# Layer kernel on one core: first values from unnormalised x, GpSimd's factors behind the copies in the sparse pairs, second sum of a norm in two halves

## The reference, cut to what matters

```python
# layer 1 (gated convolution + 16-head dilated attention)
u = rms_norm(h, norm_g)                  # y = x * rsqrt(mean(x*x) + 1e-6) * g
proj = u @ w_in                          # 10 parts of 1024 columns; part 6 is v
h = rms_norm(h + hybrid_mixer(...), final_g)
# layer 2 (12 heads, three sparse branches, and 4 memory heads)
o = gc[..., 0:1] * o_c + gc[..., 1:2] * o_s + gc[..., 2:3] * o_w     # compressed, selected, window
x = layer_norm(ALPHA * x + mix, ln1_g, ln1_b)
x = layer_norm(ALPHA * x + conv_ffn(x, ...), ln2_g, ln2_b)
# layer 3 (12 heads over blocks, 4 memory heads), same two norms
```

## Time and profile before

| | value |
|---|---|
| median of three runs | 958.37 us |
| profiled execution | 958.25 us |
| its span, first to last instruction | 956.6 us |
| TensorE busy | 928.9 us (97%) |
| VectorE busy | 659.4 us (69%) |
| ScalarE busy | 527.2 us (55%) |
| GpSimd busy | 65.6 us (7%) |
| granted TensorE clock, mean | 0.994 |

### The profile page before, as it was taken

The page is one execution under the profiler, slowest core; times in us unless marked ns, Lnnn a source line. Parts: engine busy times, 40 slices in busy tenths (PEclk is TensorE's granted clock), DMA queues, the critical chain, the costliest instruction groups (busy, mean ns, idle before and its releaser), DMA issues.

```text
span 956.6 us, 19717 instructions
## 1 busy us (share of the span) xinstructions
PE 928.9 (97%) x7025; PEld 844.7 (88%) x7025; DVE 659.4 (69%) x1258; ACT 527.2 (55%) x967; POOL 65.6 (7%) x119
## 2 busy tenths in 40 slices
PE   7999999999999999989999999999999999999995
PEld 4899999999999988667899999998988699999995
DVE  6466666666767777985886666668577796666665
ACT  5455555555544567764755455556665565555553
POOL 1000000000000001550100000001000100000001
PEclk9999999999999999999999999999999999999998
DMA  7555555556566666323566555565654447555641
GB/s 240 183 180 190 175 178 183 171 195 225 186 195 191 243 214 200 116 62 110 176 200 240 189 187 194 189 196 174 189 183 158 157 159 237 188 197 185 195 157 44
DMA packets 48233, 172.98 MB, mean 181 GB/s; under 512 B 6032, under 2 KB 6480, under 8 KB 48061
## 3 DMA queue, kind: packets, MB, share of 16 engines
q1 hardware_dynamic: 44732, 159.78, 50.7%
q0 software_dynamic: 3456, 12.61, 4.3%
HBM read 171.29 MB, written 1.07 MB: 180 GB/s over the span
## 4 chain that ended last, share of the span: by engine, by line
PE 86%; DVE 7%; ACT 3%; issue 2%; DMA 1%; POOL 0%; SPq 0%; POOLq 0%; DVEq 0%; ACTq 0%
PE bank L1411 18%; PE bank L1412 18%; PE bank L1410 18%; PE ysum L1481 6%; PE ysum L1483 6%; PE ysum L1482 6%; DVE sb_wl L830 2%; PE bank L1530 1%; PE ysum L1537 1%; PE ysum L1544 1%; PE ysum L1458 1%; PE ysum L1462 1%; PE ysum L1459 1%; DMA sb_raw<-in_stream 1%; ACT sb_xh L463 1%
## 5 line engine op out<-in xcount | busy, mean ns | idle before, releaser
L1411 PE MATMUL bank<-sb_xl,sb_wh 128*128 128x256 f32 x1360 | 377.9, 278 | 0.0
L1412 PE MATMUL bank<-sb_xh,sb_wl 128*128 128x256 f32 x1360 | 375.8, 276 | 0.0
L1410 PE MATMUL bank<-sb_xh,sb_wh 128*128 128x256 f32 x1332 | 370.5, 278 | 1.4 <-DVE sb_wl L830 1.4
L830 DVE TENSOR_TENSOR sb_wl<-sb_raw,sb_wh 128x1024 fp32r<-128x1024 f32 x201 | 245.3, 1223 | 111.9 <-ACT sb_wh L436 110.6
L436 ACT ACTIVATE sb_wh<-sb_raw 128x1024 fp32r<-128x1024 f32 x201 | 211.2, 1055 | 102.4 <-PE ysum L1483 43.4
L1410 PEld LDWEIGHTS bank<-sb_xh,sb_wh 128*128 128x128 f32 x1332 | 250.2, 188 | 6.4 <-issue 4.1
L1412 PEld LDWEIGHTS bank<-sb_xh,sb_wl 128*128 128x128 f32 x1360 | 255.5, 188 | 0.0
L1411 PEld LDWEIGHTS bank<-sb_xl,sb_wh 128*128 128x128 f32 x1360 | 255.5, 188 | 0.0
L830 DVE TENSOR_TENSOR sb_wl<-sb_gates,sb_wh 128x1024 fp32r<-128x1024 f32 x66 | 80.8, 1224 | 18.6 <-ACT sb_wh L436 18.6
L1482 PE MATMUL ysum<-sb_wl,sb_mh 128*128 128x512 f32 x208 | 81.1, 390 | 0.0
L1483 PE MATMUL ysum<-sb_wh,sb_ml 128*128 128x512 f32 x208 | 81.1, 390 | 0.0
(11 more groups left out here) (275 smaller groups left out, 1488.1 us busy)
## 6 DMA issues: line engine op xcount, KB each, us to landing
sb_raw<-in_stream SPq DMA_DIRECT2D x201, 512.0 KB, 3.4
sb_gates<-in_stream SPq DMA_DIRECT2D x66, 512.0 KB, 3.5
sb_t_dg<-in_stream SPq DMA_DIRECT2D x33, 512.0 KB, 4.1
sb_bias<-rel_rows POOLq DMA_DIRECT2D x12, 384.0 KB, 3.9
sb_bias<-in_alibi POOLq DMA_DIRECT2D x8, 256.0 KB, 3.1
sb_gb<-in_ln_g POOLq DMA_DIRECT2D x4, 512.0 KB, 5.0
sb_gb<-in_ln_b POOLq DMA_DIRECT2D x4, 512.0 KB, 6.5
sb_x_tok<-in_x SPq DMA_DIRECT2D x2, 512.0 KB, 3.7
```

The costliest lines, as they stand in the source:

```text
L830: dve.tensor_tensor(wl[slot_of(b)][:, :, :], raw[home_of(b)][:, :, :], wh[slot_of(b)][:, :, :].bitcast(F32), ALU.subtract).then_inc(split_ ...
L1410: pe.matmul(out, wh[slot][:, k, :], mov_h(k), start=k == 0, stop=False)
L1411: pe.matmul(out, wh[slot][:, k, :], mov_l(k), start=False, stop=False)
L1412: last = pe.matmul(out, wl[slot][:, k, :], mov_h(k), start=False, stop=k == KT - 1)
```

## The change

Three parts.

**Start.** TensorE turns x as it lands, not z, after 5 warm-up matmuls, and does 5 more behind the turns. xf, xh and xl are made from x times the gain, so the value products are unnormalised. VectorE writes the 1/sqrt of the tokens on a diagonal (`t_c`); behind the first value block TensorE multiplies it by ones, which puts the factor of every token on all partitions, and ScalarE copies this to `t_d`. During the value blocks VectorE multiplies xf by it and both engines split it again, slice by slice, once the value product of the slice is done. The values get their factor as they are copied out. A value block now does its matmuls by kind: four high by high (need only `wh`), four low by high, four high by low. The first dense pair stands ahead of the loop and waits for the scaled slices in its q product.

**Sparse pairs.** On VectorE the factors of the window branch come directly behind the window copies (pairs 1 to 3), or the copies come ahead of the next pair's selected factors (pairs 0 and 4). Each head's window turn has its own signal. The compressed turns stand behind the selected values' products. The window factors of pair 5 are multiplied on VectorE instead of GpSimd. ScalarE reads both turned selected heads first in pairs 4 and 5. The weight products of blocks 5 to 7 of the pairs have their first matmul in two parts.

**Norms.** Tile 1's sum is two instructions of 512 columns, the first when the first of its two banks is final. The `soon` block is made behind tile 0's scale on VectorE, and behind tile 0's square on ScalarE.

```diff
@block.gpsimd
+    pool.memset(t_b[:, 0:P], 1.0).then_inc(set_up, 1)
...
-        pool.wait_ge(S["p3", "rg"], 3 * i + 2)
+        if i < PAIRS2 - 1:
+            pool.wait_ge(S["p3", "rg"], 3 * i + 2)
...
@block.scalar
     def norm_var(nm, centred, soon=None):
...
+            if t == 0 and soon is not None:
+                refill(0, soon)
...
-    for b in range(2):
-        make_high(b)
     act.wait_ge(gains_in, 16)
-    norm_high("n0", 0, None)
+    def raw_high(k):
...
+        act.activation(xh[:, k, :], xf[:, k, :], ACT.Copy).then_inc(S["n0", "xh"], 1)
+    raw_high(0)
+    make_high(0)
+    raw_high(1)
+    make_high(1)
+    raw_high(2)
+    raw_high(3)
...
     make_high(2)
+    for k in range(4, KT):
+        raw_high(k)
+    act.wait_ge(spread, 1)
+    act.activation(t_d[:, :], bank[0][:, 0:T], ACT.Copy).then_inc(spread_s, 1)
...
+    def scaled_high(k):
+        act.wait_ge(used, k + 1)
+        act.wait_ge(p1_xm, k + 1)
+        act.activation(xh[:, k, :], xf[:, k, :], ACT.Copy).then_inc(p1_xh, 1)
     for k in range(KT - 1):
         refill(0, k)
+        scaled_high(k)
...
-    act.activation(v_all[:, 1, :], ysum[1][:, :], ACT.Copy).then_inc(v_up[0], 1)
+    act.activation(v_all[:, 1, :], ysum[1][:, :], ACT.Identity, scale=st[:, 11:12], bias=0.0
+                   ).then_inc(v_up[0], 1)
...
     def nsa(i):
+        def turned(h):
+            pt_evac("p3", i * 5 + h + 1, pt[:, 0, h, 0:CAUSAL], bank[4 + h][:, 0:CAUSAL])
-        if i == 0:
+        if i == 0 or i > 3:
+            for h in range(2):
+                turned(h)
...
@block.vector
     def norm_sum(nm, last_block, alpha, centred, x_from, fill=(), soon=None):
...
+        norm_wait(dve, nm, "half", 1)
+        ins = add_up(0, slice(0, D), 0)
...
+        norm_wait(dve, nm, "half", 2)
+        chain.link(add_up(1, slice(0, D // 2), 2))
+        dve.wait_ge(used, last_block + 1)
+        ins = add_up(1, slice(D // 2, D), 1)
...
+    def raw_fetch(k):
+        norm_wait(dve, "n0", "turned", k // 2 * 2 + 2)
+        dve.tensor_scalar(xf[:, k, :], turned_x("n0", k), gbt[:, 0, k:k + 1], None, ALU.mult
+                          ).then_inc(S["n0", "xf"], 1)
+    def raw_low(k):
+        norm_wait(dve, "n0", "xh", k + 1)
+        low(xl[:, k, :], xf[:, k, :], xh[:, k, :].bitcast(F32),
+            S["n0", "xl"])
+    def scaled(k):
+        norm_wait(dve, "n0", "xl", k + 1)
+        dve.tensor_tensor(xf[:, k, :], xf[:, k, :], t_d[:, :], ALU.mult).then_inc(p1_xm, 1)
+    def scaled_low(k):
+        dve.wait_ge(used, k + 1)
+        dve.wait_ge(p1_xh, k + 1)
+        low(xl[:, k, :], xf[:, k, :], xh[:, k, :].bitcast(F32), p1_xl)
+    raw_fetch(0)
+    raw_fetch(1)
+    raw_low(0)
+    raw_fetch(2)
+    make_low(0)
+    raw_low(1)
+    raw_fetch(3)
+    raw_low(2)
     for t in range(NT):
         norm_wait(dve, "n0", "rstd", t + 1)
-        for n in range(2):
-            part = slice(n * 512, (n + 1) * 512)
-            dve.tensor_scalar(z[:, t, part], x_tok[:, t, part], st[:, 10 + t:11 + t], None,
-                              ALU.mult).then_inc(S["n0", "z"], 1)
-    make_low(0)
-    norm_x("n0", 0, None, lambda: make_low(1))
+        dve.tensor_scalar(t_c[:, t * P:(t + 1) * P], ident[:, :], st[:, 10 + t:11 + t], None, ALU.mult
+                          ).then_inc(S["n0", "z"], 2)
+    make_low(1)
+    raw_fetch(4)
+    raw_fetch(5)
+    raw_low(3)
     make_low(2)
+    for k in range(4, KT):
+        raw_low(k)
+    dve.wait_ge(spread_s, 1)
+    scaled(0)
+    scaled(1)
     for k in range(KT - 1):
         refill(0, k)
+        if k + 2 < KT:
+            scaled(k + 2)
+        scaled_low(k)
+    scaled_low(KT - 1)
...
     def nsa(i):
+        def window_out(h):
+            dve.wait_ge(S["p3", "turned"], i * 5 + h + 3)
+            dve.tensor_copy(pt[:, 1, h, 0:CAUSAL], bank[4 + h][:, 0:CAUSAL]
+                            ).then_inc(S["p3", "pt_dve"], 1)
+        def compressed_out():
+            dve.wait_ge(S["p3", "turned"], i * 5 + 5)
...
         if i + 1 < PAIRS2:
             branch_mins(i + 1)
+            early = i in (0, 4)
+            if early:
+                for h in range(2):
+                    window_out(h)
+            branch_probs(i + 1, 0)
+            if early:
+                compressed_out()
+            selected(i + 1, 0)
+            if not early:
+                for h in range(2):
+                    window_out(h)
+                branch_probs(i + 1, 1)
+                compressed_out()
+            selected(i + 1, 1)
+            if early:
+                branch_probs(i + 1, 1)
             if i == 0:
                 refill(0, pair_at(QUERY_BLOCK[3]))
-            branch_probs(i + 1, 0)
+            branch_probs(i + 1, 2)
+            if i + 1 == PAIRS2 - 1:
+                windowed(i + 1)
...
@block.tensor
-        row_tile(slot_of(b + 1), *second, 1, False, True).then_inc(used, 1)
+        row_tile(slot_of(b + 1), *second, 1, False, True, bank_full=half).then_inc(used, 1)
...
-    warm_up(WARM_SETUP)
+    warm_up(WARM_START)
     pe.wait_ge(ident_up, 1)
-    turn_x("n0", 0)
-    turn_x("n0", 1)
+    for t in range(NT):
+        pe.wait_ge(x_in[t], 16)
+        for k in range(KT):
+            ins = pe.transpose(turned_x("n0", k)[:, t * P:(t + 1) * P], x_tok[:, t, k * P:(k + 1) * P],
+                               ident[:, :])
...
+    warm_up(WARM_START, bank[7])
+    def value_rows(k):
...
+        pe.wait_ge(split_h, k + 1)
+        norm_wait(pe, "n0", "xh", k + 1)
+        for th, _, hw, _, bk in parts:
+            pe.matmul(bk[:, :], th, hw, start=k == 0, stop=False)
+        norm_wait(pe, "n0", "xl", k + 1)
+        for _, tl, hw, _, bk in parts:
+            pe.matmul(bk[:, :], tl, hw, start=False, stop=False)
+        ready(k + 1)
+        for th, _, _, lw, bk in parts:
+            last = pe.matmul(bk[:, :], th, lw, start=False, stop=k == KT - 1)
...
+        if k == 0:
+            norm_wait(pe, "n0", "z", 4)
...
+            for t in range(NT):
+                last = pe.matmul(bank[0][:, t * P:(t + 1) * P], t_b[:, 0:P], t_c[:, t * P:(t + 1) * P],
+                                 start=True, stop=True)
...
     def nsa(i):
...
         pair_turn(i, 1)
-        pe.wait_ge(S["p3", "prob_pool"], i * 8 + 8)
-        for t in range(NT):
-            last = pe.transpose(bank[4 + t][0:32 + NCMP, CAUSAL:],
...
         for h in range(2):
             pv(h, lambda t: v_s[:, t, 0:DH], pt[:, 0, h, :], True, False)
+        pe.wait_ge(S["p3", "prob_pool"], i * 8 + (8 if i < PAIRS2 - 1 else 4))
         pe.wait_ge(S["p3", "pt_dve"], i * 4 + 2)
+        for t in range(NT):
+            last = pe.transpose(bank[4 + t][0:32 + NCMP, CAUSAL:],
...
```

More of the change, by code:

```diff
@@ L77 @@
 WARM_SETUP = 12
+WARM_START = 5
 SPLIT = 192
@@ L757, in products @@
                     refill(j, b + 4, 6)
-                    if not first:
+                    if not isinstance(j, int):
                         refill(j, b + 5, 6)
@@ L888, in norm_sum @@
                     norm_wait(dve, x_from, "x", 2)
-                for t in range(NT):
-                    if t == 0:
-                        norm_wait(dve, nm, "half", 1)
-                    else:
-                        dve.wait_ge(used, last_block + 1)
-                    ins = dve.scalar_tensor_tensor(out=z[:, t, :], in0=x_tok[:, t, :], scalar=alpha,
-                                                   in1=ysum[t][:, :], op0=ALU.mult, op1=ALU.add,
-                                                   accum_out=st[:, t:t + 1])
-                    if centred:
-                        chain.link(ins)
-                        dve.tensor_scalar(st[:, 4 + t:5 + t], st[:, t:t + 1], -1.0 / D, None,
-                                          ALU.mult).then_inc(S[nm, "mean"], 1)
-                    else:
-                        ins.then_inc(S[nm, "sum"], 1)
@@ L1402, in _, with stationary @@
         def _(pe):
-            def stationary(slot, out, mov_h, mov_l, k0=0, k1=KT, split=0):
+            def stationary(slot, out, mov_h, mov_l, k0=0, k1=KT, split=0, made=None):
                 for k in range(k0, k1):
+                    if made is not None:
+                        made(k)
                     if split and k == 0:
@@ L1483, in row_tile @@
                     last = pe.matmul(out, tl[:, t * P:(t + 1) * P], hw, start=False, stop=stop)
+                    if bank_full is not None and n == 0:
+                        last.then_inc(bank_full, 1)
                 return last
@@ new lines, in _ @@
+            warm_up(WARM_START, bank[7])
+            def value_rows(k):
+                parts = [(xh[:, k, t * P:(t + 1) * P], xl[:, k, t * P:(t + 1) * P],
+                          *(w[slot_of(k)][:, 4 * n:4 * n + 4, :].rearrange("p k c -> p (k c)") for w in (wh, wl)),
+                          bank[4 + 2 * t + n]) for t in range(NT) for n in range(2)]
+                pe.wait_ge(split_h, k + 1)
[8 more added lines that the diff above has]
```

(2 more changed lines are left out.)

161 lines of the change are left out of this document (99 added, 62 removed).

## The result

The changed kernel takes 950.48 us (median of 4 runs, 950.1 to 950.82) against 958.12 before (4 runs, 956.99 to 958.4): ratio 0.9915, 95% interval 0.9897 to 0.9932. 7.6 us are gained where 8.8 were summed, and 949.4 was forecast. The profiled execution took 950.55, with a span of 948.9.

The account below looks back on a forecast made before the run. TensorE's own work was taken as the bound (busy 928.9 of 956.6 us), so edits pay only where it stands or runs slowly. 5.5 + 1.3 + 2.0 = 8.8 off 958.25 gave 949.4, range 946.5 to 953.8.

Parts of the forecast that it names:

- Start: Time until the small product behind the value blocks: begins at 32.2 instead of 38.00; 5.5 us gained after a clock allowance.
- Pairs: Sparse pairs: 1.3 us gained together (1.35 + 0.45 - 0.5), of -0.5 to +3.
- the weights bind: Start: the first value matmul waits for the first `wh`, done at 9.23, so TensorE starts at 9.25, 1.76 us earlier.
- The warm-ups of 430.04: Sign at the end of the sparse pairs: these TensorE warm-ups come 1.3 us earlier relative to pair 0's first minimum.
- Norms: Norms n1 to n5: summing half of tile 1's columns early shortens the chain to the turns; 2.0 us gained together.
- n2, n3 and n4 ... 0.5 each: Norms: TensorE's waits at the turns and behind them, fed by the chain, shrink by 0.5 us each, of 0.2 to 0.9.
- nothing, and up to 0.6 if it is late: Norms n2 and n3: cost of the low part moved behind tile 0's scale, wanted by the second keys block.
- does nothing: Rival: the start is bound by DMA and the pairs by their loop; 958 us, chance 0.03.
- new stall: Rival, start: one late link stalls TensorE for 2.73 us again and the clock falls for 1.7; 953.8 us, chance 0.11.
- values stay at 1.2 GHz: Rival, value blocks: nothing raises the clock, so 22.4 us of work take twice that; 971.9 us, chance 0.04.
- More than summed: Rival, sparse pairs: pairs 1 to 3 shrink by 0.3 us each and pair 4 by all of 1.8; 947.6 us, chance 0.10.
- Clock starts low: Rival, start: values run at 1.2 GHz for some 4 us after fewer warm-ups; 951.7 us, chance 0.13.

Follow-up runs that it names:

- e10: The kernel before with the start part alone (value blocks, raw and rescaled slices, warm-ups): 951.79 us, ratio 0.9933.
- e1: The changed kernel with its norms part undone (one sum for tile 1, refills where they stood before): 951.52 us, ratio 0.9931.
- e2: The changed kernel with VectorE's moved low part back ahead of tile 0's scaling, half sums kept: 948.93 us, ratio 0.9903.
- e3: The changed kernel with the same low part behind tile 1's scaling, ahead of the other refills: 957.23 us, ratio 0.9988.
- e8: The changed kernel with the sparse pairs' part undone (pair 5's window factors on GpSimd, old order on TensorE, VectorE and ScalarE): 951.92 us.
- e5: The changed kernel without any warm-up matmuls, only the 16 turns of x ahead of the values: 952.31 us.
- e9: The changed kernel once more, nothing edited: 950.59 us.
- e6: The changed kernel with the five warm-ups ahead of the turns but without the five behind them: 950.61 us.

## Why the prediction was right, and which of its terms were off

**Start: 5.5 predicted, 6.2 measured** (e10; column A falls by 5.5 to 6.6 with the first warm-ups and a first value matmul before 10). The first value matmul came at 8.97, in other executions at 8.72 to 10.48, each time 0.05 behind the end of `wh`: "the weights bind" was right and the spread is the DMA's. The stall is gone, and the clock of 20 to 25 us with it. VectorE had been the stall as argued, though five fetches and seven lows stood between the two low parts, not six and eight. The small product was 6.38 earlier, 0.9 more than summed, by three terms that were too careful: 0.3 for the first matmul, 0.3 for a clock that started low and didn't, and the block's pitch, 2.75 instead of 2.80 (8 x 0.05 = 0.4), less what the two small spreading matmuls cost (0.61 us is their length, 22.65 - 8 x 2.75 = 0.65 all that is left beside the blocks, against 0.55).

**Pairs: 1.3 predicted, 0.9 to 1.2 measured** (column B, 1.11 in the changed kernel's trace). Pair 0, measured from its own minima, is 0.7 longer (predicted 0.5), pairs 1 to 3 take 26.7 to 26.9 us against 26.8 (predicted 0), and pairs 4 and 5 are 1.74 shorter (predicted 1.80). That pairs 1 to 3 did not change though TensorE's waits in them fell fits a loop of VectorE and ScalarE that binds them; no run tests it by itself. The warm-ups of 430.04 come 1.10 earlier relative to pair 0's first minimum, where 1.3 was forecast. Relative to pair 1's, at which the earlier trace rows starts, it is 1.46, but 0.4 of this is no gain: the bias block of pair 1 took 4.30 us from its issue at 370.48 to that minimum, against 3.94 before, and VectorE waited for it.

```profile
374.78 0.29 DVE L1014 CUSTOM_DVE_ANT_0 sb_sc<-bank,sb_bias 128x128 f32<-128x128 f32 x1 [1.18 <-DMA sb_bias<-rel_rows]
```

**Norms: 2.0 predicted, 0.7 (by columns N, C and D) to 1.0 measured (by e1's medians). This is the mis-sized term**, and within it "n2, n3 and n4 ... 0.5 each": they gave 0.35, -0.1 and 0 to 0.1. n1, put at nothing, gave 0.2 to 0.35. The half sum does bring the chain forward, by 0.41 (0.55 was taken; the second half costs 0.69 plus 0.2 for joining the two sums, not half of 1.22). It then meets a low part that the same edit moved behind tile 0's scaling. The prediction asked of that move only whether the low part would be late for TensorE, and took "nothing, and up to 0.6 if it is late": in n3 it was late, by 0.42. It did not ask whom VectorE would hold up meanwhile. GpSimd's step reads SBUF while VectorE subtracts two SBUF operands, and it ends 0.05 us after VectorE's instruction: 0.79 instead of 0.27 in n2, 0.82 and 0.80 in n3 and n4. e2 moves the low part and the step is short; e3 moves it the other way and it is shorter still. The Trainium skill, "SBUF — State Buffer", section "SBUF: two separate sides", states it as a rule: a VectorE instruction with two SBUF inputs and a GpSimd instruction that reads SBUF use one port pair, which the one that starts first holds to its end. The trace agrees where VectorE starts first (453.95 against 454.43 in n2). The other direction is not shown: in the kernel before VectorE's low part began at 460.65, within a GpSimd step of 460.49 to 461.06, and took its usual 1.22. n5 had no such move and keeps what the half sum gives, 8.21 - 7.79 = 0.42 from tile 0's sum to the last scaling (0.55 predicted), though there too GpSimd's two steps are long, 1.07 and 1.47 beside VectorE's instructions of 1.28 each, about as they were before.

**Sum.** 6.2 + 1.1 + 0.7 to 1.0 = 8.0 to 8.3 against 7.6 by the medians. The medians are not exact enough to close this: pairs and norms undone one by one cost 1.4 and 1.0 (e8, e1), but together they gain 1.3 over the start alone (951.79 against 950.48). From trace to trace the stages add up: 5.87 + 0.27 + 1.11 - 0.02 + 0.44 = 7.67 of 956.6 - 948.9 = 7.7, with some 0.5 lost to the matmul pitch of the changed kernel's execution. Start and norms were off in opposite directions, by 0.7 and by 1.0 to 1.3, and partly cancelled. That the total was nearer than its terms was luck. Of the rivals, "does nothing", "new stall" and "values stay at 1.2 GHz" fell with the first timeline. "More than summed" adds up to 948.05 by its own terms (949.4 - 3 x 0.3 - 0.45), not to 947.6; neither came. "Clock starts low" fell for this kernel, but e5 shows that it was real: with the turns alone the values start at 1.2 GHz and it costs 1.4 to 1.7 us, near the 1.7 of that rival's sum.

## What to carry to other kernels

Ask of every VectorE instruction that is moved which GpSimd instruction will run beside it: a 1.2 us subtraction of two SBUF operands made a 0.2 us step take 0.8 on the critical chain, and took back part of an edit that was right. The slack of such a filler ends abruptly on the other side too: against the place ahead of the chain, its middle cost 0.7 to 0.8 us in all, its end some 6 more. And price stages against a second execution of the same program before explaining a few tenths, with stages that fill the span: half a microsecond of this comparison belonged to the execution, another 0.4 to the instruction that a stage was counted from.

## What was not expected of the hardware

- A run of 256-column matmuls has a pitch of 113.5 or of 117.8 ns, mostly constant over a whole block; it can change from one block to the next with no other work between. In straight-line code either occurs, and another in the next execution of the same program (e9); in the loops of all these traces only 113.5. It sums to 2 to 3 us per execution. What sets it was not found.
- The rise of the clock is not tied to TensorE's work alone. With identical instructions the turns behind five warm-ups went from 0.21 us each to 0.11 at 5.2 us in e6 (2.41 us for 16), at other moments in other executions, and stayed slow to the last, at 7.6, in the changed kernel (3.63). Before, all twelve warm-ups passed 0.43 apart, from 2.16 to 7.2 us. The column of the granted clock says 1.00 in all of these stretches and in e5's slow value matmuls, so at the start the pitch of the matmuls has to be read instead.
- GpSimd's step on 128 x 1 elements takes 0.18 to 0.20 us alone, and as long beside the sum of a tile, which reads one operand from PSUM (452.17 in the changed kernel). Beside VectorE's scaling, SBUF to SBUF, it takes 0.27 to 0.39, beside the low part 0.80. In n2 of the kernel before, the changed one and e2 each long step ends 0.05 us behind an instruction of VectorE, so it reads as waiting and not as running slowly.
